# A state-space scan inside a two-layer mixer kernel: decays, masked scores and x times dt in two buffers, and a zero fill that is asked for later

## The reference, cut to what matters

```
seg = a_cum[:, :, :, None, :] - a_cum[:, :, None, :, :]
decay = jnp.exp(jnp.where(lower, seg, -jnp.inf))
scores = jnp.einsum('bcihn,bcjhn->bcijh', c_c, b_c) * decay * dt_c[:, :, None, :, :]
y_diag = jnp.einsum('bcijh,bcjhp->bcihp', scores, x_c)
...
y_off = jnp.einsum('bcihn,bchpn,bcih->bcihp', c_c, h_in, jnp.exp(a_cum))
```

## Time and profile before

| | us |
|---|---|
| median of 3 runs | 1500.27 (1499.72 to 1504.12) |
| profiled execution, its own time | 1498.55 |
| its span | 1496.4 |
| PE busy | 1226.1 (82% of the span) |
| DVE, ACT, POOL busy | 465.7, 264.9, 121.3 |
| layer 0's scan, first cast to last `y_norm` | 238.9 to 335.0 |
| layer 1's scan, first cast to last `y_norm` | 1016.0 to 1067.2 |

### The profile page before, as it was taken

How to read it: one execution, slowest core, us unless ns; L and a number is a source line. 1 busy time by engine, 2 the same in 40 slices (tenths; PEclk the granted TensorE clock), 3 DMA queues, 4 the chain that set the end, 5 groups by cost and what they waited for, 6 DMA issues and landing times.

```text
span 1496.4 us, 13900 instructions
## 1 busy us (share of the span) xinstructions
PE 1226.1 (82%) x5162; PEld 562.9 (38%) x5162; DVE 465.7 (31%) x1088; ACT 264.9 (18%) x564; POOL 121.3 (8%) x107
## 2 busy tenths in 40 slices
PE   3899887879998379999897299976798399788792
PEld 1363333346653123333232146533466133222231
DVE  2311444656732501111011621465562311001014
ACT  1320101114521311111010322101242111001002
POOL 2000021640000200000000200033100100000001
PEclk9899999995799689999999599986599699899995
DMA  9998109990021399999999310023003599999942
GB/s 348 379 353 310 56 0 383 420 376 2 1 74 39 161 315 378 386 382 378 388 427 339 112 56 1 0 87 137 0 8 161 188 374 387 397 402 389 424 185 91
DMA packets 86029, 347.83 MB, mean 232 GB/s; under 512 B 5958, under 2 KB 37387, under 8 KB 63435
## 3 DMA queue, kind: packets, MB, share of 16 engines
q1 hardware_dynamic: 67056, 308.76, 53.5%
q10 hardware_dynamic: 14907, 24.70, 5.0%
q0 software_dynamic: 4000, 13.49, 2.6%
HBM read 302.89 MB, written 44.04 MB: 232 GB/s over the span
## 4 chain that ended last, share of the span: by engine, by line
PE 64%; DMA 16%; DVE 13%; issue 3%; ACT 2%; POOL 1%; ACTq 1%; SPq 0%; POOLq 0%; DVEq 0%
PE ps L801 17%; PE ps L459 11%; DMA ring<-in_exp_w_up 8%; PE ps L822 7%; PE ps L726 6%; PE ps L468 5%; PE ps L402 4%; DMA ring<-in_w_mod 3%; DMA arena<-in_exp_w_up 3%; PE ps L705 2%; PE ps L424 2%; PE ps L634 1%; PE ps L680 1%; PE ps L622 1%; PE ps L677 1%
## 5 line engine op out<-in xcount | busy, mean ns | idle before, releaser
L801 PE MATMUL ps<-ring,arena 128*64 128x512 f32 x1024 | 235.3, 613 | 26.9 <-DMA ring<-in_exp_w_up 26.9
L402 PE MATMUL ps<-cst,arena 128*128 128x128 f32 x594 | 109.8, 319 | 93.6 <-DMA arena<-slots 37.4
L459 PE MATMUL ps<-u,ring 128*128 128x512 f32 (+1 forms) x416 | 168.8, 566 | 10.0 <-ACT u L1537 6.2
L1422 DVE TENSOR_TENSOR arena<-arena,ps 128x256 f32<-128x256 f32 x44 | 26.8, 610 | 421.1 <-ACT arena L1662 421.1
L402 PEld LDWEIGHTS ps<-cst,arena 128*128 128x128 f32 x594 | 76.1, 162 | 179.7 <-issue 62.3
L801 PEld LDWEIGHTS ps<-ring,arena 128*64 128x64 f32 x1024 | 72.5, 141 | 167.6 <-issue 139.1
L459 PEld LDWEIGHTS ps<-u,ring 128*128 128x128 f32 x416 | 80.2, 195 | 97.3 <-issue 91.1
L822 PE MATMUL ps<-arena 128*64 128x512 f32 x512 | 115.4, 592 | 0.9 <-ACT arena L1666 0.9
L801 PE MATMUL ps<-arena 128*64 128x512 f32 x384 | 91.7, 633 | 15.2 <-DMA arena<-in_exp_w_up 15.2
L726 PE MATMUL ps<-u,ring 128*128 128x512 f32 (+1 forms) x256 | 83.1, 486 | 1.0 <-DVE u L1266 1.0
L468 PE MATMUL ps<-ring,u 128*128 128x256 f32 (+1 forms) x224 | 75.4, 496 | 6.9 <-DVE arena L1129 6.9
(11 more groups left out here) (252 smaller groups left out, 1174.8 us busy)
## 6 DMA issues: line engine op xcount, KB each, us to landing
ring<-in_w_mod SPq DMA_DIRECT2D x24, 2048.0 KB, 14.9
ring<-in_exp_w_gate SPq DMA_DIRECT2D x22, 2048.0 KB, 23.2
ring<-in_exp_w_up SPq DMA_DIRECT2D x22, 2048.0 KB, 28.4
arena<-in_exp_w_down SPq DMA_DIRECT2D x22, 2048.0 KB, 22.2
slots<-zeros SPq DMA_DIRECT2D x4, 6144.0 KB, 41.0
arena<-in_exp_w_gate SPq DMA_DIRECT2D x10, 2048.0 KB, 22.8
arena<-in_exp_w_up SPq DMA_DIRECT2D x10, 2048.0 KB, 28.5
u<-in_exp_w_down SPq DMA_DIRECT2D x10, 2048.0 KB, 25.7
```

The costliest lines, as they stand in the source:

```text
L402: return nc.tensor.transpose(dst, src, ident[0:n, 0:n])
L459: last = nc.tensor.matmul(bank[row:row + width, 0:T - c0], w[:, k, n:n + width], u[:, k, c0:T], start=(k == 0), stop=(k == KT - 1))
L801: last = nc.tensor.matmul(ps[BLOCK * half:BLOCK * half + BLOCK, 2 + b % 2, :].rearrange("p (s n) -> p s n", s=2), x_k, pair[:, :, a:a + 25 ...
L1422: tt(hid.rearrange("p (j c) -> p c j", j=2), silu_g.rearrange("p (c j) -> p c j", j=2), ps[:, 2 + b % 2, 256:512].rearrange("p (c j) -> p ...
```

## The change

`ew` gets a second buffer in `u` (columns 0, 1 and 6, 7, which the z projection reads last and attention writes next), `gm` one in `rt`, `xdt`'s direction 0 one in `b_tok`; `xdt`'s direction 1 stays single. Tile i uses buffer i % 2. On PE both casts of tile i + 1, with their `spare(2)` each, now stand ahead of the products of tile i; so do the turn of tile i - 1 and the scores of tile i + 1. On DVE the clamps of tile i + 1 and its masks stand ahead of the sums of tile i, and the single spare part of a tile moves behind its gating. ACT takes the exponents of tile i + 1 ahead of tile i's square. On POOL the rows of tile 1 are built once z has been projected, ahead of the weights of tile 0, and the rows of tile i + 1 behind the weights of tile i and the products of tile i - 1. Separately, SP asks for the zero fill behind chunk 31 instead of ahead of chunk 8.

```
 PE
+                scores(0)
+                cast_rows(0)
+                for i, t in enumerate(tiles):
+                    if i + 1 < len(tiles):
+                        cast_rows(i + 1)
+                    if i:
+                        y_transposes(l, t - 1, i)
+                    if i + 1 < len(tiles):
+                        scores(i + 1)
                     if i == 0:
                         pe.wait_ge(S("states_done"), l + 1)
                     else:
                         pe.wait_ge(S("y_banks_read", l), i)
                     for d in range(2):
+                        pe.wait_ge(S("xdt_ready"), 2 * tiles_before(l) + 2 * i + d + 1)
                         pe.wait_ge(S("w_ready", l), 2 * i + d + 1)
...
                     last.then_inc(S("y_summed", l), 1)
-                    if i > 0:
-                        y_transposes(l, t - 1, i)
                     spare(1)
 DVE
+                masked_scores(0)
+                for d in range(2):
+                    clamp(0, d)
+                    spare(2)
+                for i, t in enumerate(tiles):
                     for d in range(2):
+                        if i + 1 < len(tiles):
+                            clamp(i + 1, d)
                         if i and d == 0:
                             y_norm(l, t - 1)
+                        if i + 1 < len(tiles):
+                            spare(2)
                     if i:
                         y_turned(l, t - 1)
+                    if i + 1 < len(tiles):
+                        masked_scores(i + 1)
                     dve.wait_ge(S("y_summed", l), i + 1)
...
                     tt(y_acc, y_acc, z[:, t, :], ALU.mult).then_inc(S("y_gated", l), 1)
+                    spare(1)
 POOL
+                rows(0)
+                pool.wait_ge(filled, entry[f"state{l}{len(state_steps(l)) - 1}"] + 1)
+                x_dt(0, 0)
+                x_dt(0, 1)
+                skip(0)
+                pool.wait_ge(filled, max(entry[f"z{l}{t}"] for t in tiles) + 1)
+                rows(1)
+                weights(0)
+                x_dt(1, 0)
+                for i in range(1, len(tiles)):
+                    weights(i)
+                    pool.wait_ge(S("y_summed", l), i)
+                    x_dt(i, 1)
+                    if i + 1 < len(tiles):
+                        rows(i + 1)
+                        x_dt(i + 1, 0)
+                    pool.wait_ge(S("y_gated", l), i)
+                    skip(i)
 SP
             for key in chunks:
-                if key == ("in", 0, "z", 0):
-                    sp.wait_ge(S("zeros_ready"), 1)
-                    for k in range(ZERO_DMAS):
...
                 load(ring_at[key], key)
...
+            sp.wait_ge(S("zeros_ready"), 1)
+            for k in range(ZERO_DMAS):
...
             experts(0)
```

More of the change, by code:

```diff
@@ L252, in hybrid_dit_kernel, with xdt_of @@
         y_skip = take(512)
+        ews = [[ew[:, d] for d in range(2)],
+               [u[:, k:k + 2, :].rearrange("p k t -> p (k t)").rearrange("p (h i) -> p h i", i=P) for k in (0, 6)]]
+        gms = [gm, rt[:, 0:8, :, :].rearrange("p s t e -> p (s t e)").rearrange("p (d g i) -> p d g i", d=2, i=P)]
+        b_tok_row = b_tok.rearrange("p t n -> p (t n)")
+        def xdt_of(i, d):
+            return b_tok_row if d == 0 and i % 2 else xdt[:, d, :]
         sc = take(64 * 12).rearrange("p (k n) -> p k n", n=64)
@@ L606, in scan_tiles, with scores @@
             def scan_tiles(l):
-                first = FIRST_T[l]
-                for i, t in enumerate(range(first, TT)):
+                tiles = range(FIRST_T[l], TT)
+                def scores(i):
+                    t = tiles[i]
                     for g in range(2):
@@ L1135, in scan_tiles, with masked_scores @@
             def scan_tiles(l):
[L1136 to L1139, removed]
+                tiles = range(FIRST_T[l], TT)
+                def masked_scores(i):
+                    if i >= 2:
+                        dve.wait_ge(S("w_ready", l), 2 * (i - 1))
                     for g in range(2):
-                        bank = claim(f"cb{l}{t}{g}")
+                        bank = claim(f"cb{l}{tiles[i]}{g}")
@@ L1142, in scan_tiles, with clamp @@
                         for d in range(2):
-                            last = tt(gm[:, d, g, :], bank[:, 0:P], tri[d], ALU.mult)
+                            last = tt(gms[i % 2][:, d, g, :], bank[:, 0:P], tri[d], ALU.mult)
                         emptied(last)
-                    for d in range(2):
[L1146 to L1153, removed]
+                def clamp(i, d):
+                    dve.wait_ge(S("rows_cast", l), 2 * i + d + 1)
+                    for hh in range(SSD_H):
+                        last = ts(ews[i % 2][d][:, hh, :], ps[:, 2 + hh // 4, P * (hh % 4):P * (hh % 4) + P],
+                                  sc[:, 8, 32 * d + 8 * tiles[i] + hh:32 * d + 8 * tiles[i] + hh + 1], 0.0,
+                                  ALU.subtract, ALU.min)
+                    last.then_inc(S("decay_clamped", l), 1)
@@ L1780, in _, with rows @@
                         S("xde_ready", l), 1)
-                for i, t in enumerate(range(first, TT)):
+                tiles = range(first, TT)
+                def rows(i):
                     for d in range(2):
[L1784 to L1798, removed]
-                    pool.wait_ge(evacuated, entry[f"cb{l}{t}1"] + 1)
```

53 lines of the change are left out of this document (35 added, 18 removed).

## The result

The changed kernel takes 1526.56 us (median of 4 runs, 1521.18 to 1534.5) against 1502.19 us for the kernel before on the same chip (4 runs, 1499.72 to 1509.35): a ratio of 1.0165, interval 1.0135 to 1.0195. It is slower by 1.65%; the forecast was 1516 with a range from 1503 to 1527. The profiled execution took 1530.82 us, its span is 1529.0.

A forecast was written before the change was run, and what follows sets the result against it. No engine bounds the kernel everywhere; each scan's own chain counts, with transfers in layer 0's. Zero fill 0, layer 0 +14.0 and layer 1 +1.5 make +15.5 on 1498.55, 1514.1, or 1516 on the median's scale; range 1503 to 1527.

The forecast's parts named there:

- the forecast's own upper bound of 18: Layer 0's scan: cost in us if short idle times in each cycle let the clock fall a few times; 14.0 expected.
- the third rival: Scan cycles: clock falls in most pauses, each cast 1.7 us slower, attention recovers it later; 1526 us; chance 0.13.
- The zero fill at 0: SP's queue: moving the fill behind chunk 31 costs 0, covered by attention; up to 60 us without that cover.
- Tile 0's products at 272.6: Layer 0: products stand behind tile 1's casts and parts and wait for chunk 19, starting 15.4 us later than 257.24.
- The cycle of 24.1 us: Layer 0, tiles 1 and 2: products start to products start takes 24.1 us against 21.0 before.
- the forecast's likeliest case: Whole kernel: about 1516 us, layer 0 costing 14.0 with low clock only in its last products; forecast's chance 0.66.
- the clamp at 2.2 us: Layer 0's cycle: DVE's clamp behind the first cast counted as 2.2 us of the 24.1.
- The last tile: Layer 0: last products wait for tile 2's tail, PE idle some 4.5 us, products 9.5 us at 1.2 GHz, end 348.7 to 349.0.
- Layer 1 at +1.5: Layer 1's scan: -3.4 us from overlap, 2.7 price beside DVE's rotations, up to +7.2 at 1.2 GHz; +1.5 taken.
- Attention passed on whole: Attention behind each layer's scan: starts after the last y_norm, so a shift there is passed on whole.
- rival 1: PE's clock holds through the last products into layer 0's attention, saving 13.4 us there; 1491.5 us in total; chance 0.11.
- rival 2: No change: tile 0's late start is caught up by cycles of 17 to 18 us; 1499 to 1504 us; chance 0.10.

The follow-up runs named there:

- the parts at 1, 1 and 3: Changed kernel with a tile's five modulation parts placed one behind each cast and three behind the products; 1507.98 us, ratio 1.0031 to the kernel before.
- The run with the turn behind the products: Changed kernel with the last tile's products ahead of the turn of the tile before, in each layer; 1513.44 us, ratio 1.0086 to the kernel before.
- the five profiles of the same program in layer 1: Kernels sharing the changed layer 1: layer 1 alone, parts behind the products, full change, scan's order alone, parts 1, 1, 3; scans 47.7 to 54.1 us.
- The kernel with the scan's order alone: Changed kernel with the zero fill back ahead of chunk 8; 1529.15 us, ratio 1.0182 to the kernel before.
- all mends: Changed kernel with parts 1, 1 and 3, layer 1's tile 1 rows after the rotations, last turn behind the last products; 1500.37 us, ratio 0.9991 to before.

## Why the prediction was right, and where it was not

The direction was right (slower had 0.79), and the mechanism was right in its order of steps. 1516 was 10.6 us too low, and 1526.56 lies 0.4 us inside the range, which is luck: the same scan with the fill in its old place measured 1529.15. The change was +24.4 us by the medians and +32.3 by the two profiled executions, on which the sum was built, where the forecast had +15.5. Layer 0 alone came out at +21.2, above the forecast's own upper bound of 18.

The time is that of the third rival (1526, chance 0.13), and its mechanism came in part. The clock did fall in pauses of both cycles, and attention got it back later. But the casts of the two cycles cost 0 to 0.8 us more each and not 1.7, and about as much again was DVE's, which that rival does not name.

**The zero fill at 0.** Right: by itself the late fill measured 0.9989, with 1 inside the interval. Attention hid it, and the stretch with the experts behind it did not get longer.

**Tile 0's products at 272.6.** They started at 273.02. They waited for chunk 19, as the step had it: PE used it at 270.75 after 1.42 us of waiting for the transfer. The lower bound, an earlier chunk, did not come.

**The cycle of 24.1 us: mis-sized, it was 27.6.** The order of the steps was right, and their parts can be laid against the timeline above. Products to first cast: 9.2 forecast, 9.4 measured. Cast to clamp's end: 4.2 forecast, 5.5 measured (282.39 to 287.85), for DVE's stretched sums and the copy ahead. Placing: 0.7 and 0.55. One chunk: 1.9 and 3.6. Second cast: 2.0 and 2.75. Two chunks 3.64 and 3.6, turn and second score 2.4 and 2.3. Of the 3.5 us missing, 2.4 are the chunk and the second cast at 1.2 GHz and 1.3 the later clamp. The later clamp has two causes that overlap: the first cast's own low clock would account for 0.8, and DVE, busy with stretched sums and the copy, for all 1.3. In the second cycle the clamp ended 6.9 us after its cast began, for 4.2; that cast ran at the full clock, so these 2.7 us are DVE's alone. The chunk and the second cast cost 2.0 more there, and the steps ahead of the first cast 0.7 less. Two cycles make +7.1, nearly all by which layer 0 missed (20.0 and the 1.2 us ahead of the scan, for 14.0).

So two terms of the cycle failed, and they weigh about the same: 4.4 us of the two cycles are the clock, 4.0 the clamps.

The first is the premise behind the forecast's likeliest case, that idle times under the 2.69 us of the earlier trace rows do no harm. After 2.32, 0.69 and 1.44 us the clock was low here. The kernel before had already shown it one cycle later:

```profile
293.66 2.51 PE L622 MATMUL ps<-arena,ones 128*128 128x512 f32 x4 [2.52 <-DVE arena L1150]
```

This cast took 2.51 us after 2.52 us of idle time, and one at 316.24 took 1.96 after the same 2.52. Nor does a longer idle time decide: the chunk of the earlier trace rows took 1.92 us after 3.06 us of waiting, and in the changed kernel it took 3.34 after the same 3.06. The length of one pause was not enough to forecast from.

The second is the clamp at 2.2 us behind its cast, which takes DVE to be free. "Sums, exponents and weights lie beside it now" was the forecast, but on DVE the sums of a tile stand ahead of the clamp of the tile after next, and POOL's rows for that tile run beside them. The forecast priced POOL beside DVE for the rotations of layer 1 (2.7 us) and in the last tile (0.3 us), and at nothing in the cycles. There three sums took 4.8 and 5.4 us where they take 2.1 alone. No run kept POOL away from these sums, so their share is read from the timeline and was not tested. The run with the parts at 1, 1 and 3 has the same stretched sums in a cycle of 22.6 us: they cost little where PE has other work until DVE is free.

**The last tile.** The interval from tile 2's products to the last ones was forecast as 12.3 us and was 12.3; from there to `y_norm`'s end 15.8 and 15.6. Idle 4.35 us for "some 4.5", passes of 3.52 and 3.67 us. The run with the turn behind the products shows it by its absence: 8.0 and 12.9 us.

**Layer 1 at +1.5.** It was +1.9 in this profile. The price beside the rotations was forecast as 2.7 and measured as 3.0 to 3.2: two operations of 2.09 and 2.00 us instead of 0.41 and 0.42. Each of the two lasts about as long as one of POOL's two instructions (3.93 / 2). The Trainium skill, page "SBUF — State Buffer", section "SBUF: two separate sides", describes these shared ports as an exclusive lock that is held for a whole instruction. The trace agrees in kind, and the price lies between my 2.7 from rows and the 3.8 that I had estimated with that rule. The scan's gain of 3.4 came in four profiles (47.7 to 47.8 us for 51.2). It was 1.3 in the full change, where tile 1's casts took 3.75 and 3.36 us for 1.96 and 2.96, and nothing or less in two others of the same program. Counted from the mixer's start to the last `y_norm`, where this profile has +2.9, the five profiles of the same program in layer 1 range from -0.6 to +6.3; that +1.9 met +1.5 is in part luck.

**Attention passed on whole.** Not quite: +4.0 and +4.2 us. In layer 0 the clock was 0.50 for 63.8 us from the last `y_norm` on and not 56. The kernel with the scan's order alone also took 94.9 us for the whole, and the others took 88.0 to 93.2 with scans that end otherwise. In layer 1 it is different: the scan's order alone took 52.8 with the same program for which the full change took 56.9. So layer 0's part goes with the order, by two profiles only, and layer 1's varies from run to run. What decides when the clock comes back in attention was not tried and stays open.

**The rivals.** The clock did not hold into attention (rival 1): 0.50 from 340.6 on. Nor would it have been enough to hold it in the scan: with all mends the last products ran at the full clock (2.00 us), and attention still ran at 0.50 for its first 55 us and took 91.0. The late start was not caught up (rival 2), though with the parts at 1, 1 and 3 the loss fell to 0.3%: whether the parts fit into waits that are there anyway was a matter of where they stand.

## What to carry to other kernels

When one engine's hand-written order is changed for overlap, write the cycle down engine by engine with every handshake in it, also those of filler work: here the second buffers cost nothing once the rest was mended (0.9991), and gained nothing either; what cost the time was two matmul parts between two casts, a turn ahead of the last products, and a clamp behind sums that another engine stretches. Price such a cycle twice, at the full and at the low TensorE clock, and read every cycle of the trace before, not one: the low clock stood in the second of three here. Expect the same program to differ by some us from profile to profile. Filler work belongs where its engine waits anyway, in portions small enough that no handshake inside it outlasts the wait.

## What the runs showed of the hardware that was not expected

- The granted clock can be low after short idle times: a chunk took 3.64 us instead of 1.92 after idle times of 2.32, 0.69 and 1.44 us, whereas in the earlier trace rows a cast after 2.69 us still took 1.96. The same pause can do both: in one profile of the kernel before, casts after 2.52 us took 2.51 and 1.96 us. Casts with the same pauses of 2.34 to 2.35 us took 1.96 in one kernel's profile and 3.03 in another's with the same program up to there.
- In layer 0's attention of the changed kernel PE was busy 60.7 of 63.8 us at 0.50 before the clock rose to 1.00. The score products of 512 keys stand on both sides of that rise, as in the earlier trace rows.
- DVE sums with both inputs in SBUF took 1.00 to 2.45 us beside POOL's work for 0.69 alone; one with one input in PSUM was not stretched (0.69 at 280.62 and at 309.64).
- In the kernel with the zero fill alone, zeros moved at 355 GB/s and a DMA share of 1.05 over the first 56 us of layer 0's attention, and left its length as it was (91.06 us against 90.9).
